# The first four norms: transposing the raw residual and applying the root after the projections

## The chip, the cores and the metric

One Trainium2 chip, one of its cores, one launch. The metric is the device time of that launch in microseconds (us), median of several runs. PE is TensorE (the matrix engine), DVE is VectorE, ACT is ScalarE, POOL is GpSimd, SP is SyncE, which here only issues transfers. SBUF is the on-chip memory that the engines work in, PSUM the eight accumulator banks (128 x 512 f32 each) that PE writes.

## What is computed

A stack over 256 tokens of width 1024, all in float32: retention, gated FFN with a convolution, stick-breaking attention, the same FFN again, a norm, and then a second block (adaptive norm, mLSTM and block attention, mixture of experts). The first four norms, which the change touches, stand ahead of the projections of the first four parts.

```python
def _rmsnorm(x, g):
    xf = x.astype(jnp.float32)
    y = xf * lax.rsqrt(jnp.mean(xf * xf, axis=-1, keepdims=True) + EPS)
    return (y * g.astype(jnp.float32)).astype(x.dtype)

def _retention(h, w_in, w_out):
    ...
    proj = h @ w_in
    ...
    y = jax.nn.silu(g.astype(jnp.float32)) * o
    return y.astype(h.dtype) @ w_out

def _conv_ffn(h, w_up, conv_w, conv_b, w_down):
    u = h @ w_up
    u = lax.conv_general_dilated(u, conv_w[:, None, :].astype(u.dtype), window_strides=(1,),
                                 padding=[(CONV_W - 1, 0)],
    ...
    gate, val = jnp.split(u, 2, axis=-1)
    return (jax.nn.silu(gate) * val) @ w_down

    for i in range(DEPTH):
        j = i // N_MIXERS
        if i % N_MIXERS == 0:
            x = x + _retention(_rmsnorm(x, ret_norm[j]), ret_w_in[j], ret_w_out[j])
        else:
            x = x + _stick_breaking(_rmsnorm(x, sb_norm[j]), sb_w_in[j], sb_w_out[j])
        x = x + _conv_ffn(_rmsnorm(x, ffn_norm[i]), ffn_w_up[i], ffn_conv_w[i],
                          ffn_conv_b[i], ffn_w_down[i])
```

DEPTH is 2: retention stands in the first round, stick-breaking in the second. The factor rsqrt(mean(x*x) + EPS), called the root here, is one number per token. A projection of the normed tokens is therefore the projection of x times g, with each token's outputs multiplied by its root.

## The kernel before

**Products in three passes.** Every weight and every normed activation is split into a rounded high part and a low part (type fp32r), and a product is made as high x high, high x low and low x high. ACT makes the high part of a weight half (`split_high`, L443), DVE the low part (`split_low`, L451), each in two pieces of 128 x 1024. Of the split weights there are two buffers, `w_high` and `w_low`, so the split of half h+2 can begin only when PE is through with half h. A half is 48 matmuls of 256 columns (`by_feature`, L514 to L516; features on partitions, tokens along the columns) or 24 of 512 columns (`by_token`, L529 to L531; tokens on partitions).

**A norm.** ACT squares and sums each 128-token tile as the residual is added (L302), DVE makes mean plus EPS (L309), ACT the square root (L305), DVE the reciprocal (L312) and then the scaled tiles `xn` (L321). PE transposes them by 16 matmuls against the identity into banks 0 to 3 (L337), ACT takes the high part of the transposed tokens times g (L364, eight of 128 x 256) and DVE the low part (L366). The first matmul of the projection waits for the first of four pairs of L366. Ahead of norms 1 and 3 PE runs five matmuls whose result nobody reads (`idle_turns`, L327, 128 x 512); ahead of norm 2 it sums the adaptive gates (L1009, four of 128 x 512).

**After a projection.** Retention's q and k come out with tokens along the columns and DVE rotates them by the cos and sin tables (L1820 to L1824); v and gate come out with tokens on partitions and are copied (ACT L1464, DVE L1831). In the FFN ACT takes a bank of PSUM times the third tap plus the bias (L1528), DVE adds the other two taps in four instructions that read the same bank (L1906, L1912), ACT applies silu (L1534) and DVE multiplies (L1920). In the first FFN PE puts four matmuls of the adaptive weights (`ada_part`, L954) behind every half. Both FFNs have 22 halves.

**Order.** Each engine has one program in order; semaphores join them. SP issues all weight transfers on one queue: ident (the identity), the two halves of x, the first 256 columns of the first weight unit, `small` (gains, biases, taps), the rest of that unit, unit 1 (halves 2 and 3), and from then on unit n when the halves that lay in its slot are split. The other constants, of 576 KB, and the tables for decay, cos and sin, of 1280 KB, are issued behind that wait of unit 2 (L757, L758). DVE waits for them (L1813, L1814) ahead of the splits of the third half. `rqk_free` and `up_free` count the banks that are free again, `norm_xn` the scaled tiles, `x_new` the halves of residual tiles.

## Time and profile before

| | |
|---|---|
| time, median of 3 runs | 1430.35 us (1430.11 to 1430.64) |
| the profiled execution | 1430.92 us, of which its span 1429.2 us |
| PE busy | 1360.0 us, 95% of the span |
| DVE busy | 709.8 us, 50% |
| ACT busy | 557.9 us, 39% |
| POOL busy | 33.9 us, 2% |
| mean granted clock of PE | 0.985 |
| chain that ended last | PE 81%, DVE 7%, DMA 7%, ACT 3%, issue 2% |

Busy shares are means over stages with different limits. The chain is the work that ended last, followed back from the last instruction: in most of the span it lies on PE, and the other engines appear in it where PE stood still for them. Matmuls overlap, so a matmul's listed duration is longer than the distance to the next.

### The profile page before, as it was taken

To read this page: it belongs to the slowest core of one execution; us is meant where nothing else is said; L and a number is where in the kernel's file an instruction comes from. 1 tells how busy PE (TensorE), PEld (TensorE's weight loads), DVE (VectorE), ACT (ScalarE), POOL (GpSimd) and SP (SyncE) were. 2 spreads that over 40 slices of the span, in tenths; PEclk is the share of its full clock that TensorE was granted. 3 is DMA by queue.
4 is the path that set the end of the run, shared out by engine and by line. 5 is a ranking of instruction groups with operands and counts; after the bars stand their busy time and mean duration, and the time that the engine had idled before them with its cause. 6 is when DMAs were issued, how large, how long until landed. Compare 5 with 4: busy or idle time off the path is not lost.

```text
span 1429.2 us, 20105 instructions
## 1 busy us (share of the span) xinstructions
PE 1360.0 (95%) x7982; PEld 983.2 (69%) x7982; DVE 709.8 (50%) x1242; ACT 557.9 (39%) x855; POOL 33.9 (2%) x54
## 2 busy tenths in 40 slices
PE   6999899999999998999999998898999999999996
PEld 6988587888777997899987776764444444444442
DVE  5754546666646444577765765852223223222222
ACT  4344535555545466556554644521111111111111
POOL 1000000111100000000000000000000000000000
PEclk9999999999999999999999999999999999999998
DMA  9557343989943642255645343189999999999994
GB/s 316 180 206 257 118 147 104 311 294 316 354 156 120 209 172 85 68 177 176 236 178 203 111 140 118 60 313 416 427 428 426 430 427 428 429 427 430 428 428 179
DMA packets 112286, 372.64 MB, mean 261 GB/s; under 512 B 4300, under 2 KB 63980, under 8 KB 99552
## 3 DMA queue, kind: packets, MB, share of 16 engines
q1 hardware_dynamic: 104352, 344.07, 62.6%
q0 software_dynamic: 7872, 27.76, 5.7%
q8 instruction: 37, 0.61, 0.2%
q14 instruction: 25, 0.20, 0.0%
HBM read 370.75 MB, written 1.05 MB: 260 GB/s over the span
## 4 chain that ended last, share of the span: by engine, by line
PE 81%; DVE 7%; DMA 7%; ACT 3%; issue 2%; SPq 0%; ACTq 0%; DVEq 0%
PE ps L552 14%; PE ps L1353 13%; PE ps L514 9%; PE ps L515 8%; PE ps L516 8%; PE ps L1374 7%; DMA arena<-in_w_expert_up_dram 5%; PE ps L1336 4%; PE ps L529 3%; PE ps L530 3%; PE ps L531 3%; DVE w_low L451 2%; PE ps L954 2%; PE ps L1380 1%; ACT w_high L443 1%
## 5 line engine op out<-in xcount | busy, mean ns | idle before, releaser
L451 DVE TENSOR_TENSOR w_low<-ring,w_high 128x1024 fp32r<-128x1024 f32 x264 | 311.5, 1222 | 225.6 <-ACT w_high L443 217.2
L443 ACT ACTIVATE w_high<-ring 128x1024 fp32r<-128x1024 f32 x264 | 264.9, 1052 | 228.1 <-PE ps L552 95.1
L514 PE MATMUL ps<-h_high,w_high 128*128 128x256 f32 x1088 | 313.9, 289 | 4.4 <-DVE w_low L451 2.9
L515 PE MATMUL ps<-h_low,w_high 128*128 128x256 f32 x1088 | 309.3, 284 | 0.0
L516 PE MATMUL ps<-h_high,w_low 128*128 128x256 f32 x1088 | 309.1, 284 | 0.0
L514 PEld LDWEIGHTS ps<-h_high,w_high 128*128 128x128 f32 x1088 | 210.2, 193 | 25.0 <-issue 20.9
L515 PEld LDWEIGHTS ps<-h_low,w_high 128*128 128x128 f32 x1088 | 210.3, 193 | 0.0
L516 PEld LDWEIGHTS ps<-h_high,w_low 128*128 128x128 f32 x1088 | 210.1, 193 | 0.0
L1353 PE MATMUL ps<-ring,arena 128*64 128x512 f32 x592 | 176.6, 594 | 6.4 <-issue 1.5
L1353 PEld LDWEIGHTS ps<-ring,arena 128*64 128x64 f32 x592 | 55.4, 137 | 117.4 <-issue 111.8
L552 PE MATMUL ps<-w_high,h_high 128*128 128x512 f32 x304 | 95.8, 397 | 4.7 <-DVE h_low L467 3.0
L1353 PE MATMUL ps<-arena 128*64 128x512 f32 x336 | 98.9, 594 | 0.6 <-DMA arena<-in_w_expert_up_dram 0.6
L552 PE MATMUL ps<-w_low,h_high 128*128 128x512 f32 x304 | 94.2, 391 | 0.0
L552 PE MATMUL ps<-w_high,h_low 128*128 128x512 f32 x304 | 94.1, 391 | 0.0
L1374 PE MATMUL ps<-ring,arena 128*64 128x512 f32 x320 | 92.1, 595 | 0.9 <-ACT arena L1757 0.7
L529 PE MATMUL ps<-w_high,h_high 128*128 128x512 f32 x208 | 82.8, 398 | 2.1 <-DVE w_low L451 1.5
L530 PE MATMUL ps<-w_low,h_high 128*128 128x512 f32 x208 | 81.5, 392 | 0.0
L531 PE MATMUL ps<-w_high,h_low 128*128 128x512 f32 x208 | 81.5, 392 | 0.0
L1745 ACT ACTIVATE arena<-ps,mods 128x128 f32<-128x128 f32 x64 | 24.1, 456 | 134.0 <-PE ps L1336 134.0
L1336 PEld LDWEIGHTS ps<-arena,xn 128*128 128x128 f32 x512 | 61.0, 196 | 15.1 <-issue 12.2
L552 PEld LDWEIGHTS ps<-w_high,h_high 128*128 128x128 f32 x304 | 56.6, 190 | 21.0 <-issue 7.2
L1764 ACT ACTIVATE y_high<-arena 128x512 fp32r<-128x512 f32 x32 | 19.7, 631 | 127.9 <-DVE arena L2355 127.9
(339 smaller groups left out, 1599.5 us busy)
## 6 DMA issues: line engine op xcount, KB each, us to landing
ring<-in_ffn_w_up_dram SPq DMA_DIRECT2D x44, 1024.0 KB, 7.9
ring<-in_w_expert_gate_dram SPq DMA_DIRECT2D x19, 2048.0 KB, 28.6
ring<-in_w_expert_down_dram SPq DMA_DIRECT2D x18, 2048.0 KB, 27.0
ring<-in_w_expert_up_dram SPq DMA_DIRECT2D x18, 2048.0 KB, 26.0
ring<-in_ret_w_in_dram SPq DMA_DIRECT2D x11, 2048.0 KB, 8.0
arena<-in_w_expert_up_dram SPq DMA_DIRECT2D x11, 2048.0 KB, 27.8
ring<-in_ffn_w_down_dram SPq DMA_DIRECT2D x10, 2048.0 KB, 7.9
arena<-in_w_expert_gate_dram SPq DMA_DIRECT2D x10, 2048.0 KB, 25.3
```

Of the source, the lines that this page charges most:

```text
L443: nc.scalar.activation(hi, raw, ACT.Copy).then_inc(hi_done, 1)
L451: last = eng.tensor_tensor(lo, raw, hi.bitcast(F32), ALU.subtract)
L514: nc.tensor.matmul(o, hi, hTh[:, k, :], start=(k == 0), stop=False)
L515: nc.tensor.matmul(o, hi, hTl[:, k, :], start=False, stop=False)
L516: last = nc.tensor.matmul(o, lo, hTh[:, k, :], start=False, stop=(k == KD - 1))
L529: nc.tensor.matmul(o, hi, wh[:, row, :], start=(k == 0), stop=False)
L530: nc.tensor.matmul(o, hi, wl[:, row, :], start=False, stop=False)
L531: last = nc.tensor.matmul(o, lo, wh[:, row, :], start=False, stop=(k == KD - 1))
L552: last = nc.tensor.matmul(ps[:, 4 + 2 * t + half, :], a, w[b][:, cols], start=(first and c == 0), stop=(end and c == 2))
L1336: last = nc.tensor.matmul(ps[:, 4 + half, (k % 4) * P:(k % 4 + 1) * P], xn[:, t, k * P:(k + 1) * P], sel[:, t, :], start=(t == 0), stop=(t ...
L1353: last = nc.tensor.matmul(ps[e * R:(e + 1) * R, 4 + g, :], xg[:, k, e * R:(e + 1) * R], wide[homes[e]][:, k, :], start=(k == 0), stop=(k = ...
L1374: last = nc.tensor.matmul(ps[e * R:(e + 1) * R, 6 + half, :], hgT[:, k, e * R:(e + 1) * R], tall[homes[e]][:, k, half * C:(half + 1) * C], ...
```

## The change

**Norms 0 to 3.** PE transposes the residual itself (`late_pe`), tile by tile and half by half as `x_new` counts them, and ACT and DVE split its product with g as before. The squares of tile 0 stand ahead of ACT's high parts, those of tile 1 and the square root behind the split of the second weight half. DVE then makes the reciprocal and, by two multiplications of the identity, a diagonal matrix of the roots for each tile (`root_diag`). After the second half of the projection (the third in `sb_v`) PE multiplies it by ones into bank 7, which gives the roots along the columns on every partition (`late_rows_pe`, two matmuls of 128 columns), and DVE copies that to `root_rows` (128 x 256).

**Where the root is applied.** In `ret_qk` DVE multiplies cos and sin by the row once. In `ret_vg` and `sb_v` the copies out of PSUM carry the root as a scale. In `sb_qk` the copies become products with the row. In the FFNs DVE writes the bank times the row to `us` in SBUF (128 x 512, one instruction more per half), and taps, bias and convolution read `us`; the bank is free after that one instruction. The row is read only after the splits of half 2, ahead of the evictions of half 0, since it is made after half 1.

**Beside it.** `idle_turns` is three matmuls of 256 columns, behind the transposes. The gate sums of norm 2 are two behind the transposes and two behind half 0 of `sb_v`. SP issues the first weight half ahead of x, and constants and tables ahead of the wait of unit 2. ACT's first function is a copy, so that the table for the square root is loaded behind the first weight split. PE's loop for `ret_qk` and the first round of the FFN loops are written out, as is DVE's FFN loop.

```diff
+        LATE = 4
+        R_BANK = 7
+        root_rows = [carve(14400 if r == 0 else 15000, T) for r in range(LATE)]
+        root_diag = [carve(14656 if r == 0 else 15256, NT, P) for r in range(LATE)]
...
+        def x_ready(eng, r, t, half):
+
+            if r == 0:
+                eng.wait_ge(x_in[t], 16)
+            else:
+                eng.wait_ge(x_new, update(r - 1) - 4 + 2 * t + half + 1)
...
+        def late_square(act, r, t):
+
+            if t == 0:
+                if r == 0:
+                    act.wait_ge(ident_in, 16)
+                nc.scalar.activation(credit[:, 7:8], const[:, 0:1], ACT.Sqrt)
+            x_ready(act, r, t, 1)
+            nc.scalar.activation(xn[:, t, :], x[:, t, :], ACT.Square, accum_out=stat[:, t:t + 1]).then_inc(norm_ss, 1)
+
+        def late_sqrt(act, r):
+            act.wait_ge(norm_ms, r + 1)
+            nc.scalar.activation(stat[:, 4:6], stat[:, 2:4], ACT.Sqrt).then_inc(norm_sd, 1)
+
+        def late_root(dve, link, r):
+
+            dve.wait_ge(norm_ss, NT * (r + 1))
+            nc.vector.tensor_scalar(stat[:, 2:4], stat[:, 0:2], 1.0 / D, EPS, ALU.mult, ALU.add).then_inc(norm_ms, 1)
+            dve.wait_ge(norm_sd, r + 1)
+            link(nc.vector.reciprocal(stat[:, 6:8], stat[:, 4:6]))
+            for t in range(NT):
+                last = nc.vector.tensor_scalar(root_diag[r][:, t, :], ident, stat[:, 6 + t:7 + t], None, ALU.mult)
+            last.then_inc(norm_xn, 1)
+
+        def late_rows_pe(pe, r):
+
+            pe.wait_ge(norm_xn, r + 1)
+            for t in range(NT):
+                last = nc.tensor.matmul(ps[:, R_BANK, t * P:(t + 1) * P], ones, root_diag[r][:, t, :], start=True, stop=True)
+            last.then_inc(norm_rows, 1)
+
+        def late_rows(dve, link, r):
+            dve.wait_ge(norm_rows, r + 1)
+            link(nc.vector.tensor_copy(root_rows[r], ps[:, R_BANK, 0:T]))
+
+        def across(r, n=2):
+            return root_rows[r].unsqueeze(1).broadcast_to([P, n, T])
+
+        def late_pe(pe, r):
+
+            for t in range(NT):
+                for j in range(4):
+                    x_ready(pe, r, t, j // 2)
+                    for k in (2 * j, 2 * j + 1):
+                        last = nc.tensor.transpose(ps[:, j, (k % 2) * T + t * P:(k % 2) * T + (t + 1) * P],
+                                                   x[:, t, k * P:(k + 1) * P], ident)
+                    if t == NT - 1:
+                        last.then_inc(norm_tr, 1)
...
             sp.dma_start(const[:, 0:P], A["const"][:, 0:P]).then_inc(ident_in, 16)
+            first = rows(A["ret_w_in"][0])
+            sp.dma_start(wide[0][:, :, 0:T], first[:, :, 0:T]).then_inc(first_in, 16)
             sp.dma_start(x[:, 0, :], x_tiles[:, 0, :]).then_inc(x_in[0], 16)
             sp.dma_start(x[:, 1, :], x_tiles[:, 1, :]).then_inc(x_in[1], 16)
-            first = rows(A["ret_w_in"][0])
-            sp.dma_start(wide[0][:, :, 0:T], first[:, :, 0:T]).then_inc(first_in, 16)
...
-                if before[n] is not None:
-                    sp.wait_ge(*freed[before[n]])
                 if n == 2:
                     sp.dma_start(const[:, P:], A["const"][:, P:NKEPT]).then_inc(const_in, 16)
                     sp.dma_start(arena[:, ARENA - NCONST + NKEPT:], A["const"][:, NKEPT:]).then_inc(tables_in, 16)
+                if before[n] is not None:
+                    sp.wait_ge(*freed[before[n]])
...
-            norm_pe(pe, 0)
...
+            late_pe(pe, 0)
+
+
+            for h in range(8):
+                buf = split_ready(pe, "ret_qk", h)
+                if h >= 4:
+                    pe.wait_ge(rqk_free, h - 3)
+                by_feature(h % 4, buf, None if h else 0).then_inc(wide_mm, 1)
+                if h == 1:
+                    pe.wait_ge(const_in, 16)
+                    late_rows_pe(pe, 0)
...
+                        if isinstance(i, int) and h == 1:
+                            late_rows_pe(pe, 2 * l + 1)
+
+                four(0)
+                with pe.Fori(1, 5) as i:
+                    four(i)
...
-            norm_pe(pe, 1, 5)
+            late_pe(pe, 1)
+            idle_turns(3, 4, T)
             pe.wait_ge(ada_c, 1)
-            pe.wait_ge(const_in, 16)
             ffn(0)
...
+            def gate_sums(g, q):
                 for half in range(2):
                     last = nc.tensor.matmul(ps[:, 4 + 2 * g + half, :], ones,
                                             ada_acc[:, q * D + half * C:q * D + (half + 1) * C],
                                             start=True, stop=True)
-            last.then_inc(ada_gsum, 1)
-            norm_pe(pe, 2)
+                last.then_inc(ada_gsum, 1)
+
+            pe.wait_ge(ada_ev, 2 + NB)
+            late_pe(pe, 2)
+            gate_sums(0, 2)
 
 
             for h in range(4):
                 buf = split_ready(pe, "sb_v", h)
                 by_token(2 * (h // 2), buf, h % 2, 2 if h < 2 else None).then_inc(wide_mm, 1)
+                if h == 0:
+                    gate_sums(1, 5)
+                if h == 2:
+                    pe.wait_ge(ada_gate, 4)
+                    late_rows_pe(pe, 2)
...
-            norm_act(act, 0)
+            act.wait_ge(ident_in, 16)
             nc.scalar.activation(credit[:, 3:4], const[:, 0:1], ACT.Copy).then_inc(rvg_fa, 2)
             split_high(act, "ret_qk", 0)
+            late_square(act, 0, 0)
             act.wait_ge(small_in, 16)
             split_norm(act, 0, 0)
             split_high(act, "ret_qk", 1)
+            late_square(act, 0, 1)
+            late_sqrt(act, 0)
             for h in range(2, count["ret_qk"]):
                 split_high(act, "ret_qk", h)
+            act.wait_ge(norm_xn, 1)
...
-                                             ACT.Copy).then_inc(rvg_fa, 1)
+                                             ACT.Identity, scale=stat[:, 6:7]).then_inc(rvg_fa, 1)
...
+                    act.wait_ge(up_free, off + ((FP + 4) * l + 4 + 2 * b + j + 1))
                     for gv in range(2):
                         at = (l * 2 + gv) * FP
                         last = nc.scalar.activation(
-                            cv[:, j, gv * T:(gv + 1) * T], ps[:, (2 * b + j) % 4, gv * T:(gv + 1) * T], ACT.Identity,
+                            cv[:, j, gv * T:(gv + 1) * T], us[:, j, gv * T:(gv + 1) * T], ACT.Identity,
...
+            def late_norm(r, phase):
+                split_high(act, phase, 0)
+                late_square(act, r, 0)
+                split_norm(act, r, 0)
+                split_high(act, phase, 1)
+                late_square(act, r, 1)
+                late_sqrt(act, r)
+
+            late_norm(1, "up0")
...
-            norm_dve(dve, link, 0)
-            dve.wait_ge(small_in, 16)
-            nc.vector.memset(credit[:, 0:1], 0.0).then_inc(rqk_free, 4)
-            nc.vector.memset(credit[:, 2:3], 0.0).then_inc(rvg_fv, 2)
             nc.vector.memset(hT[:, 0, :], 0.0).then_inc(ada_zero, 1)
             split_low(dve, "ret_qk", 0)
+            dve.wait_ge(small_in, 16)
             split_norm(dve, 0, 1)
             split_low(dve, "ret_qk", 1)
+            late_root(dve, link, 0)
             cos, sin = k_("cos"), k_("sin")
-            dve.wait_ge(const_in, 16)
-            dve.wait_ge(tables_in, 16)
             for q in range(8):
                 u = ps[:, q % 4, :]
                 split_low(dve, *(("ret_qk", q + 2) if q < 6 else ("ret_vg", q - 6)))
+                if q == 0:
+                    late_rows(dve, link, 0)
+                    dve.wait_ge(tables_in, 16)
+                    for table in (cos, sin):
+                        pair_of = table.rearrange("p (b t) -> p b t", b=2)
+                        link(nc.vector.tensor_tensor(pair_of, pair_of, across(0), ALU.mult))
+                    nc.vector.memset(credit[:, 2:3], 0.0).then_inc(rvg_fv, 2)
...
+                def pair(n):
+                    c, u = cv[:, n % 2, :], us[:, n % 2, :]
...
+                    def scaled():
+                        wide_done(dve, halves[f"up{l}"] + n + 1)
+                        nc.vector.tensor_tensor(u.rearrange("p (b t) -> p b t", b=2),
+                                                ps[:, n % 4, :].rearrange("p (b t) -> p b t", b=2), across(r), ALU.mult)\
+                            .then_inc(up_free, 1)
+
+                    if n:
+                        scaled()
+                    if n + 2 < FP:
+                        split_low(dve, f"up{l}", n + 2)
+                    elif n + 2 == FP:
+                        split_low(dve, f"down{l}", 0)
                     else:
...
+                        src_low(dve, f"down{l}", hff, 0)
+                        split_low(dve, f"down{l}", 1)
+                        src_low(dve, f"down{l}", hff, 1)
+                    if n == 0:
+                        late_rows(dve, link, r)
+                        scaled()
+                    dve.wait_ge(up_id, FP * l + n + 1)
+                    dve.wait_ge(up_free, (FP + 4) * l + 4 + n + 1)
...
+                    dve.wait_ge(up_si, FP * l + n + 1)
                     nc.vector.tensor_tensor(hff[:, n, :], c[:, 0:T], c[:, T:C], ALU.mult).then_inc(up_h, 1)
...
+                for n in range(FP):
+                    pair(n)
```

The order on ACT at the start of the program, before; `credit` is a scratch column, `stat` holds the sums and roots:

```order
L299 ACT_TABLE_LOAD
L299 ACTIVATE credit<-const 128x1
L302 ACTIVATE xn,stat<-x_hT 128x1024 x2
L305 ACTIVATE stat<-stat 128x2
L1450 ACTIVATE credit<-const 128x1
L443 ACTIVATE w_high<-ring 128x1024 x2
L364 ACTIVATE h_high<-ps,small 128x256 x8
```

The same place in the changed kernel, with its own line numbers:

```order
L1526 ACT_TABLE_LOAD
L1526 ACTIVATE credit<-const 128x1
L502 ACTIVATE w_high<-ring 128x1024 x2
L312 ACT_TABLE_LOAD
L312 ACTIVATE credit<-const 128x1
L314 ACTIVATE xn,stat<-x_hT 128x1024
L423 ACTIVATE h_high<-ps,small 128x256 x8
L502 ACTIVATE w_high<-ring 128x1024 x2
L314 ACTIVATE xn,stat<-x_hT 128x1024
L318 ACTIVATE stat<-stat 128x2
```

The weight split now stands ahead of a second table load and of one square; the other square and the root have moved behind the second split.

The order on DVE in `ret_qk`, before, from the splits of the second and third half to that of the fourth:

```order
L451 TENSOR_TENSOR w_low<-ring,w_high 128x1024 x4
L1820 TENSOR_TENSOR xn<-ps,arena 128x512
L1821 TENSOR_TENSOR xn<-ps,arena 128x256
L1822 TENSOR_TENSOR xn<-ps,arena 128x256
L1824 TENSOR_TENSOR arena<-xn 128x512
L451 TENSOR_TENSOR w_low<-ring,w_high 128x1024 x2
```

The first row ends with the split of the third half, behind which the first rotation follows. The changed kernel, from the split of the third half on:

```order
L510 TENSOR_TENSOR w_low<-ring,w_high 128x1024 x2
L339 COPY arena<-ps 128x256
L1902 TENSOR_TENSOR arena<-arena 128x512 x2
L1903 MEMSET credit 128x1
L1905 TENSOR_TENSOR xn<-ps,arena 128x512
L1906 TENSOR_TENSOR xn<-ps,arena 128x256
L1907 TENSOR_TENSOR xn<-ps,arena 128x256
L1909 TENSOR_TENSOR arena<-xn 128x512
L510 TENSOR_TENSOR w_low<-ring,w_high 128x1024 x2
```

Between the split and the first rotation the copy of the row and the two table products have come in.

The order on DVE at the start of the first FFN, before, where the last rows are the loop's first evictions:

```order
L366 SCALAR_TENSOR_TENSOR h_low<-ps,small,h_high 128x256 x8
L451 TENSOR_TENSOR w_low<-ring,w_high 128x1024 x2
L1922 UNCONDITIONAL_BRANCH
L1922 ISA
L451 TENSOR_TENSOR w_low<-ring,w_high 128x1024
L450 REGISTER_ALU
L451 TENSOR_TENSOR w_low<-ring,w_high 128x1024
L1903 ISA
L1906 ISA
L1906 SCALAR_TENSOR_TENSOR arena<-ps,small,arena 128x255
```

The split of half 2 is followed by the evictions of half 0. The changed kernel, from the diagonal matrices on:

```order
L327 TENSOR_SCALAR arena<-const,stat 128x128 x2
L510 TENSOR_TENSOR w_low<-ring,w_high 128x1024 x2
L339 COPY arena<-ps 128x256
L1980 TENSOR_TENSOR arena<-ps,arena 128x512
L2003 SCALAR_TENSOR_TENSOR arena<-arena,small 128x255 x2
L2003 SCALAR_TENSOR_TENSOR arena<-arena,small 128x254 x2
L2012 TENSOR_TENSOR arena<-arena 128x256
L1980 TENSOR_TENSOR arena<-ps,arena 128x512
L510 TENSOR_TENSOR w_low<-ring,w_high 128x1024 x2
L2003 SCALAR_TENSOR_TENSOR arena<-arena,small 128x255 x2
```

The split of half 3 (the second L510) stands behind the whole eviction of half 0, and that stands behind the copy of the row (L339), which PE makes after half 1.

## Rows read from the trace of the kernel before

**Rows 1.** page: busy time of an engine; then GB/s in 40 equal slices

```profile
PE 1360.0 (95%) x7982; PEld 983.2 (69%) x7982; DVE 709.8 (50%) x1242; ACT 557.9 (39%) x855; POOL 33.9 (2%) x54
...
GB/s 316 180 206 257 118 147 104 311 294 316 354 156 120 209 172 85 68 177 176 236 178 203 111 140 118 60 313 416 427 428 426 430 427 428 429 427 430 428 428 179
```

**Rows 2.** waits of PE, whole span: engine line <- releaser: us in total, times, longest

```profile
PE ps L337 <- DVE xn L321: 11.1, 4, 9.9
```

**Rows 3.** timeline of the start: start us, us, engine line op out<-in xcount [idle <-releaser]

```profile
0.87 1.28 ACT L299 ACT_TABLE_LOAD   x1 [0.87 <-PEq L2448]
...
5.21 1.06 ACT L302 ACTIVATE xn<-x_hT 128x1024 f32<-128x1024 f32 x1 [2.16 <-DMA x_hT<-in_x_dram]
...
9.54 2.00 ACT L443 ACTIVATE w_high<-ring 128x1024 fp32r<-128x1024 f32 x2 [1.30 <-DMA ring<-in_ret_w_in_dram]
...
9.94 3.64 PE L337 MATMUL ps<-const,xn 128*128 128x128 f32 x16 [9.94 <-DVE xn L321]
...
10.64 2.35 DVE L451 TENSOR_TENSOR w_low<-ring,w_high 128x1024 fp32r<-128x1024 f32 x2
...
11.45 3.01 ACT L364 ACTIVATE h_high<-ps,small 128x256 fp32r<-128x256 f32 x8
...
12.91 3.22 DVE L366 SCALAR_TENSOR_TENSOR h_low<-ps,small,h_high 128x256 fp32r<-128x256 f32 x8
...
13.92 0.55 PE L514 MATMUL ps<-h_high,w_high 128*128 128x256 f32 x1 [0.34 <-DVE h_low L366]
```

**Rows 4.** timeline of the first projection, tables and the fifth weight half

```profile
18.81 0.43 SPq L758 DMA_DIRECT2D arena<-in_const_dram  x1
...
26.76 2.36 DVE L451 TENSOR_TENSOR w_low<-ring,w_high 128x1024 fp32r<-128x1024 f32 x2 [8.37 <-DMA arena<-in_const_dram]
...
31.15 2.36 DVE L451 TENSOR_TENSOR w_low<-ring,w_high 128x1024 fp32r<-128x1024 f32 x2
...
36.84 2.01 ACT L443 ACTIVATE w_high<-ring 128x1024 fp32r<-128x1024 f32 x2 [8.43 <-DMA ring<-in_ret_w_in_dram]
```

**Rows 5.** two windows of 10 us: window, length, busy (x) by engine, PEclk, DMA share, GB/s

```profile
26.00:36.00 10.00, 7.13 (x48) 6.93 (x47) 8.64 (x12) 2.00 (x2) 1.60 (x3) 0.83 1.03 340
...
903.00:913.00 10.00, 7.39 (x59) 6.64 (x57) 5.63 (x10) 1.97 (x3) 0.00 (x0) 1.00 0.05 20
```

**Rows 6.** timeline around norm 1, PE, DVE and ACT

```profile
224.49 4.45 PE L327 MATMUL ps<-const 128*128 128x512 f32 x10
...
224.69 1.29 DVE L576 TENSOR_TENSOR x_hT<-ps,x_hT 128x512 f32<-128x512 f32 x2 [0.73 <-PE ps L552]
...
229.30 1.97 PE L337 MATMUL ps<-const,xn 128*128 128x128 f32 x16 [0.36 <-DVE xn L321]
...
230.00 3.02 ACT L364 ACTIVATE h_high<-ps,small 128x256 fp32r<-128x256 f32 x8 [2.40 <-PE ps L337]
...
231.90 0.35 PE L514 MATMUL ps<-h_high,w_high 128*128 128x256 f32 x1 [0.62 <-DVE h_low L366]
```

**Rows 7.** timeline around norm 2, PE and DVE

```profile
451.65 3.67 PE L1009 MATMUL ps<-arena,const 128*128 128x512 f32 x8 [1.47 <-DVE x_hT L576]
...
457.69 0.47 PE L529 MATMUL ps<-w_high,h_high 128*128 128x512 f32 x1 [0.62 <-DVE h_low L366]
...
462.08 2.48 DVE L1958 TENSOR_TENSOR gates<-ps,gates 128x512 f32<-128x512 f32 x4
```

**Rows 8.** timeline of one up-projection half of the second FFN, ACT and DVE

```profile
600.44 2.01 ACT L443 ACTIVATE w_high<-ring 128x1024 fp32r<-128x1024 f32 x2 [1.76 <-PE ps L516]
...
602.36 1.00 ACT L1528 ACTIVATE arena<-ps,small 128x256 f32<-128x256 f32 x2
...
605.34 0.42 ACT L1534 ACTIVATE arena<-arena 128x256 f32<-128x256 f32 x1 [1.98 <-DVE arena L1912]
...
601.53 2.36 DVE L451 TENSOR_TENSOR w_low<-ring,w_high 128x1024 fp32r<-128x1024 f32 x2 [2.92 <-ACT w_high L443]
...
607.25 1.23 DVE L451 TENSOR_TENSOR w_low<-ring,w_high 128x1024 fp32r<-128x1024 f32 x1 [0.85 <-ACT w_high L443]
```

124 lines of the change are left out of this document (43 added, 81 removed).

## Prediction

> **What bounds the kernel now.** I read the page first: PE is busy 95% of the span, DVE half of it [rows 1]. So time is won only where PE stands still, runs work that nobody needs, or runs at the lower clock, and I went on to the waits of PE: the transposes of the norms waited 11.1 us in four pieces for DVE's scaled tiles, 9.9 of them at the start [rows 2]. The timelines then show what PE does around each norm. At norm 1 the projection's last matmul is followed at 224.49 by five idle turns, then by the transposes at 229.30, and the first useful matmul starts at 231.90, 7.4 us later [rows 6]. Norm 3 has the same form. At norm 2 the gate sums fill part of the same chain [rows 7]. At the start the first matmul is at 13.92 [rows 3], and halves 2 and 3 of `ret_qk` suffer from the tables: DVE waits 8.37 us for them ahead of the split at 26.76 [rows 4]. From 26 to 36 us PE is busy 7.13 of 10 us, idle for 2.87, at a mean granted clock of 0.83 [rows 5].
>
> **Start and `ret_qk`.** Landings: tile 0 of x was there at 5.21 and the first weight half at 9.54, 1.5 MiB in 4.33 us between them [rows 3]. With the weight half (1 MiB) in place of tile 0 (0.5 MiB) at the head, it lands at about 5.21 + 1.44 = 6.65. ACT's split takes 2.00, to 8.65; the second table load 1.28, to 9.95; one square 1.06 with some tenths around it; so ACT begins the high parts at 11.4, where it began before at 11.45 [rows 3]. The table load eats what the earlier weight gives. But DVE's low weight part, which ran from 10.64 for 2.35 and held L366 back to 12.91, is now done by 10.1. In norm 1 the first matmul comes 1.90 behind ACT's first high part (230.00 to 231.90) [rows 6]; here that is 13.3: **-0.6**. The transposes run earlier, with a longer hole behind them. At the start 16 of them took 3.64 us, against 1.97 in norm 1, so PE was at the lower of its two clock levels (1.2 GHz); I charge **+0.3** for a later rise, with ends at -0.7 and +2.
>
> The tables now follow unit 1 in the queue and land before they are needed. The idle 2.87 goes, and with it the low clock: 0.17 of 10 us [rows 5], **-2.87** and **-1.7**. In their place stands the row. Two 128-column products cost PE what its idle turns show: ten records in 4.45 us are five matmuls of 512 columns [rows 6], so 128 columns take 0.22 and two 0.45: **+0.45**. Behind it DVE copies the row (about 0.4), multiplies two tables (about 0.7 each, with waits 1.6 together) and rotates, which takes 2.03 (29.12 to 31.15), and only then splits half 3 in 2.36 [rows 4]. With hand-over times that is 6.8 us behind the row, and PE has half 2 for 5.72 of them (601.53 to 607.25, one half's period) [rows 8]: a new wait of **+1.05**. Sum of this stage: -3.4. On the clock of the run: half 1 ends at 26.0, half 2 at 32.2, half 3 starts at 33.25 and ends at 39.0.
>
> **Norm 1.** Residual tile 0 is ready when the projection ends, so eight transposes run from 224.5 to 225.5. DVE adds tile 1 in two pieces from 224.69 to 225.98 [rows 6]; each piece releases four transposes of 0.12. The first pair is done at 225.8, ACT starts at 226.0, and 1.90 later, at 227.9, the projection can start. PE ends its transposes at 226.7 and runs three turns of 256 columns, 1.33 us, to 228.05. Against 231.90 that is **-3.85**; the idle turns cost 0.15 of it. The row adds **+0.45**.
>
> Then comes what the change adds by its order. DVE reads the row only after half 1, and behind it stand the eviction of half 0 and the split of half 3, on DVE and on ACT both. I lay it from the row matmuls' start R. Row copied at R+1.1; scaled bank at R+1.9; ACT's bias pass from R+2.1. From that pass to silu took 2.98 before (602.36 to 605.34), silu 0.42, from ACT's split to DVE's 1.09 (600.44 to 601.53), DVE's split 2.36 [rows 8]. Half 3 is ready at R+8.9. PE has 0.45 for the row, 5.72 to 5.9 for half 2 and, in this FFN, 1.0 for the adaptive weights: it arrives at R+7.4. **+1.5**. Norm 1 gives -1.9.
>
> **Norm 2.** The same chain, but the gate sums are real work of 3.67 us [rows 7]. Half of them now runs while ACT and DVE split, so with the transposes done at 452.2 (as in norm 1, 2.2 behind the projection) and two sums of 1.84 together the first product starts at 454.05; the other half (1.84) and the row (0.45) follow it: 456.35 in place of 457.69, **-1.35**. DVE adds the gates (2.48, [rows 7]) behind the second half of the sums and ahead of a weight split, which costs PE 0 to 0.7; I take +0.05. -1.3.
>
> **Norm 3.** -3.85 and +0.45 as in norm 1; without adaptive weights PE arrives at R+6.2 and waits **+2.65**: -0.75. Whether PE comes back at the lower clock is open: after 2.87 idle it did, after 2.61 (903 to 913 us, clock 1.00) it did not [rows 5]. The price was 1.7; the new gap lies between the two, and I take half: **+0.85**. +0.1 for norm 3.
>
> **Steady state.** The FFNs get one DVE instruction more per half, 0.6 us apart from its neighbour. In the second FFN DVE stood idle for 0.85 ahead of a split in a period of 5.72 [rows 8], so it fits by 0.25, and the first FFN has 1.0 more. Scaled copies in `ret_vg`, `sb_v` and `sb_qk` take the place of unscaled ones; I take them at nothing, covered by PE's halves, with +1 as the upper end. The experts' stage streams weights at 427 GB/s [rows 1]; its first loads are released by work behind the norms, so it moves forward with them.
>
> **Sum.** -3.4 - 1.9 - 1.3 + 0.1 = -6.5. The profiled execution took 1430.92, a span of 1429.2 and 1.7 around it; it lies 0.6 above the median, so the same difference taken from the median 1430.35 gives **1423.8**.
>
> **The rivals.**
>
> *The waits behind the row are smaller, or low-clock stretches elsewhere vanish.* If ACT and DVE catch up within half 2, the three waits (1.05, 1.5, 2.65) and the clock term fall away by half or more: -6.5 - 3 to -6, 1418 to 1421. Against it: in-order queues, and each term of the chain comes from a row. Chance 0.12.
>
> *The row's waits cost clock too.* Three new gaps of 1 to 2.7 us, the hole at the start, and all later gaps shifted against the clock's changes: each fall costs 1.7 [rows 5]. Two more give 1427.2, and 1426 to 1428.5 is this case's range. Chance 0.15.
>
> *The fifth weight half is late.* In the trace it was issued after the tables and ACT could start on it only at 36.84, after an idle 8.43 [rows 4], with POOL's transfers in flight. If it lands there again, it is split 3.45 later, at 40.3, while PE now wants it at 39.0: +1.3, 1425.1. For it: POOL's transfers do not move. Against it: the tables are out of the way, 1280 KB that were ahead of it. Chance 0.10. The Trainium skill, page "DMA: Bandwidth & Descriptors", section "Queues, rings and completion order", says that a DMA engine takes turns between the queues that have work, packet by packet; by that rule POOL's queue keeps its share whatever SP puts ahead, which is this rival, and its sum would be -5.2. No row separates the two queues' shares here.
>
> *The experts' stream swallows it.* If the 427 GB/s stretch [rows 1] ended at a fixed time, the end would stay at 1430.4. Against it: nothing ties it to a time, each slot is refilled when PE has used it. Chance 0.05.
>
> *Slower.* DVE becomes the bound of the second FFN: `scaled` reads a repeated row and PSUM and stands between silu's product and the next split, on a loop of ACT and DVE that has 0.25 to spare. If the loop's period grows beyond 5.72 by d, PE loses d in each of some 19 halves behind the first wait. To lose the 6.5 and 2.9 more, d must be 0.5, so `scaled` would have to cost 0.75 more than the 0.6 that I give it, over 1.35. Two-input instructions of 128 x 1024 cost 1.18 a piece [rows 8], so 512 columns at half that rate would just reach it. Chance 0.04.
>
> **Chances and range.** The forecast itself, 1421.5 to 1426, has 0.54; the five rivals 0.12, 0.15, 0.10, 0.05 and 0.04. A measurement of this kernel can tell about 0.2%, 2.9 us, from no change. Faster by more than that, below 1427.5: 0.54 + 0.12 + 0.10 + two thirds of 0.15, less a little for what I have not seen, 0.85; within it 0.11; slower 0.04. The range 1419.5 to 1427.5 takes in the late half, most of the clock case, half of the small waits, and leaves out about 2 in 10.
>
> **What would show it.** In the profile of the changed kernel: the first product near 13.3; no idle PE and full clock at 26 us, but a wait of about 1 us ahead of half 3 of `ret_qk`; the first product of norm 1 3.85 us earlier against the projection's end; a wait of 1.5 us ahead of half 3 in the first FFN and of 2.65 in the second, with the clock falling behind the second or not; DVE some 13 us busier in 22 halves of each FFN, with no PE wait in the steady state. If PE waits for DVE's low part in every half of the second FFN, the slower case holds; if PE's gaps are gone and the end has not moved, the experts' stream held it. I am wrong in the sum if any wait behind the row is off by more than 1 us.

## The result, and the profile of the changed kernel

The changed kernel takes **1419.17 us** (median of 4 executions, 1417.32 to 1419.43), the kernel before beside it 1430.23: ratio 0.992, 95% interval 0.9907 to 0.9932. The forecast was 1423.8 with a range from 1419.5. So the sign was right, the gain of 11.1 us was 1.7 times the forecast 6.5, and the time lies 0.3 us under the range. With the later repetitions it is 1419.36 over 15 executions against 1430.57 over 56.

The page of the changed kernel: its span, the busy time of the engines, and GB/s in 40 slices.

```profile
span 1417.5 us, 19885 instructions
...
PE 1353.1 (95%) x7990; PEld 981.7 (69%) x7990; DVE 738.1 (52%) x1291; ACT 562.7 (40%) x856; POOL 33.3 (2%) x54
...
GB/s 318 206 204 241 122 145 129 323 310 320 341 166 132 212 146 60 76 192 187 248 166 178 134 119 119 60 342 419 426 427 427 429 428 428 429 429 428 429 428 192
```

PE's busy time fell by 6.9 of the 11.7 us that the span lost, and DVE's grew by 28.3 [rows 1]. The experts' stream has the same 427 GB/s and simply ends earlier.

**The start**, timeline of the changed kernel (start us, us, engine, operation):

```profile
6.80 2.00 ACT L502 ACTIVATE w_high<-ring 128x1024 fp32r<-128x1024 f32 x2 [2.48 <-DMA ring<-in_ret_w_in_dram]
...
8.26 3.65 PE L350 MATMUL ps<-const,x_hT 128*128 128x128 f32 x16 [8.26 <-DMA x_hT<-in_x_dram]
8.82 1.28 ACT L312 ACT_TABLE_LOAD   x1
...
11.27 3.01 ACT L423 ACTIVATE h_high<-ps,small 128x256 fp32r<-128x256 f32 x8
...
13.22 0.55 PE L573 MATMUL ps<-h_high,w_high 128*128 128x256 f32 x1 [1.32 <-DVE h_low L425]
```

The weight is split from 6.80 (forecast 6.65), the high parts begin at 11.27 (11.4), the first product at 13.22 (13.3), against 13.92 in [rows 3]. Behind it the clock rises later than before: the matmuls of 256 columns, 0.21 us apart at first, come 0.12 apart from 15.48 on in the kernel before and from 17.20 on in the changed one (timelines of PE, before and then changed):

```profile
15.13 0.40 PE L516 MATMUL ps<-h_high,w_low 128*128 128x256 f32 x1
...
15.48 0.28 PE L515 MATMUL ps<-h_low,w_high 128*128 128x256 f32 x1
15.60 0.28 PE L516 MATMUL ps<-h_high,w_low 128*128 128x256 f32 x1
```

```profile
16.77 0.41 PE L574 MATMUL ps<-h_low,w_high 128*128 128x256 f32 x1
16.99 0.37 PE L575 MATMUL ps<-h_high,w_low 128*128 128x256 f32 x1
17.20 0.28 PE L573 MATMUL ps<-h_high,w_high 128*128 128x256 f32 x1
```

In this the same matmuls go from 0.70 ahead of before to 0.41 behind. The granted clock does not show it: the profile gives 1.00 from 12 to 19 us in both traces, though a distance of 0.21 is what the same matmuls have near 601 us, where it shows the lower level.

**`ret_qk`**, timelines of DVE, PE and ACT:

```profile
22.15 2.36 DVE L510 TENSOR_TENSOR w_low<-ring,w_high 128x1024 fp32r<-128x1024 f32 x2 [3.42 <-ACT w_high L502]
27.20 0.42 DVE L339 COPY arena<-ps 128x256 f32<-128x256 f32 x1 [2.69 <-PE ps L334]
27.66 1.42 DVE L1902 TENSOR_TENSOR arena<-arena 128x512 f32<-128x512 f32 x2
...
31.32 2.36 DVE L510 TENSOR_TENSOR w_low<-ring,w_high 128x1024 fp32r<-128x1024 f32 x2
...
33.74 0.39 PE L573 MATMUL ps<-h_high,w_high 128*128 128x256 f32 x1 [0.83 <-DVE w_low L510]
...
39.86 2.01 ACT L502 ACTIVATE w_high<-ring 128x1024 fp32r<-128x1024 f32 x2 [4.84 <-PE ps L575]
```

The tables no longer stand ahead of the split of half 2 (at 22.15 where it was at 26.76), the row is copied at 27.20, and with the table products and the rotation behind it this holds the split of half 3 back to 31.32; PE waits 0.83 for it. The split at 39.86 is that of the fifth half: released by PE, not by a transfer as at 36.84 in [rows 4]. That weight is not late.

**The norms.** Norm 1, then norm 2, then the two places of norm 3 with its first product in the kernel before (the row of L514), all timelines:

```profile
219.65 2.20 PE L350 MATMUL ps<-const,x_hT 128*128 128x128 f32 x16
219.85 1.29 DVE L635 TENSOR_TENSOR x_hT<-ps,x_hT 128x512 f32<-128x512 f32 x2 [0.74 <-PE ps L611]
...
221.07 3.03 ACT L423 ACTIVATE h_high<-ps,small 128x256 fp32r<-128x256 f32 x8 [0.77 <-PE ps L350]
...
221.69 1.46 PE L386 MATMUL ps<-const 128*128 128x256 f32 x6
...
222.96 0.36 PE L573 MATMUL ps<-h_high,w_high 128*128 128x256 f32 x1
```

```profile
442.74 2.20 PE L350 MATMUL ps<-const,x_hT 128*128 128x128 f32 x16
...
444.78 1.88 PE L1076 MATMUL ps<-arena,const 128*128 128x512 f32 x4
...
446.10 0.80 PE L588 MATMUL ps<-w_high,h_high 128*128 128x512 f32 x1
```

```profile
579.88 0.35 PE L573 MATMUL ps<-h_high,w_high 128*128 128x256 f32 x1
...
600.12 0.39 PE L573 MATMUL ps<-h_high,w_high 128*128 128x256 f32 x1 [2.17 <-DVE w_low L510]
```

```profile
594.14 0.35 PE L514 MATMUL ps<-h_high,w_high 128*128 128x256 f32 x1 [0.62 <-DVE h_low L366]
```

In norm 1 the first product starts 3.3 us behind the transposes' first, where it was 7.4 behind the projection's end [rows 6]. Against the matmuls ahead of it, it moved forward by 4.08 in norm 1, 4.30 in norm 2 (half of whose gate sums now follow it) and 4.06 in norm 3.

**The clock.** Busy time, length and granted clock (the number behind POOL's) of four windows of the changed kernel; then of two of the kernel before:

```profile
26.00:36.00 10.00, 9.17 (x77) 8.97 (x76) 8.46 (x15) 4.02 (x4) 2.00 (x4) 1.00 0.78 239
175.00:185.00 10.00, 8.97 (x40) 7.47 (x41) 4.76 (x7) 4.20 (x7) 0.62 (x1) 1.00 0.38 131
550.00:560.00 10.00, 10.00 (x54) 8.63 (x53) 4.78 (x5) 6.90 (x9) 0.00 (x0) 1.00 0.00 1
600.00:606.00 6.00, 5.88 (x36) 5.88 (x37) 5.80 (x11) 3.30 (x5) 0.00 (x0) 0.72 0.82 265
```

```profile
175.00:185.00 10.00, 7.69 (x26) 6.22 (x27) 4.47 (x8) 2.67 (x5) 0.75 (x1) 0.66 0.64 239
550.00:560.00 10.00, 7.49 (x38) 5.54 (x39) 2.11 (x4) 7.88 (x10) 0.00 (x0) 0.66 0.66 210
```

This is what the forecast did not have. The kernel before runs 10 us near 176, and 10 us near 551, at a mean of 0.66: two thirds of each at the lower of the two levels (1.2 in place of 2.4 GHz), which costs up to 3.4 us each time, less where PE waits anyway. In this execution of the changed kernel the first is absent, and the second is shorter and lies at 542 (clock 0.91 from 540 to 560, against 0.83 from 545 to 565 before). The waits ahead of both are the same in both traces: 1.4 at most in the retention, and 3.2 at L1110 (before L1035).

**Where the 11.7 us went.** Shift of the same matmul from one trace to the other (profiled executions: span 1429.2 to 1417.5):

| stage | forecast | measured |
|---|---|---|
| start and `ret_qk` | -3.4 | -2.6 |
| low clock near 176 | 0 | -2.2 |
| norm 1, with its wait | -1.9 | -2.4 |
| norm 2 | -1.3 | -1.6 |
| low clock near 551 | 0 | -1.3 |
| norm 3, with wait and clock | +0.1 | +0.2 |
| from 606 us to the end | 0 | -1.8 |
| sum | -6.5 | -11.7 |

The first line is read at the first matmul of the retention, which stands behind `ret_qk` and `ret_vg` and ahead of the stretch near 176 (timelines of PE, before and changed):

```profile
152.32 1.02 PE L906 MATMUL ps<-arena 128*128 128x256 f32 x4
```

```profile
149.71 0.81 PE L969 MATMUL ps<-arena 128*128 128x256 f32 x3
```

The four stages that the forecast had priced sum to -6.4 here, almost its -6.5; the other -5.3 lie in the three lines that it had at nothing. In the last line, stretches at the low clock near 845 (-1.5), near 898 (+1.6) and near 955 (nothing in the end) almost cancel. What is left of it is mostly a wait for an expert's weights, -1.1 by shift (PE's waits, before and changed; 1.1 again in the next execution traced of the changed kernel):

```profile
PE ps L1353 <- DMA x_hT<-in_w_expert_gate_dram: 1.3, 1, 1.3
```

```profile
PE ps L1429 <- DMA x_hT<-in_w_expert_gate_dram: 0.3, 1, 0.3
```

To see this for many executions I use, for each, its span and its mean granted clock. Their product is a full-clock time: it leaves out what the lower level costs (and, a little too much, idle time within it; the clock is given to 0.001, or 1.4 us an execution). Over all executions:

| kernel | n | median us | mean us | mean clock | span x clock |
|---|---|---|---|---|---|
| before | 56 | 1430.57 | 1430.56 | 0.9859 | 1408.7 |
| changed | 15 | 1419.36 | 1419.74 | 0.9883 | 1401.4 |

Work and waits: **-7.3**. Clock: 0.0024 of 1420, **-3.4**. The forecast says -5.65 for the first and -0.85 (-1.7 + 0.85) for the second. Its +0.3 for the late rise at the start belongs to the first, since the granted clock does not show that rise.

### The profile page after: what moved, and what is told of

Its sections match the earlier page's. It is cut to its first block, busy times and chain, and to the rows that moved or that the text cites. A ratio compares the mean times of both kernels' runs of the same rounds, so it can differ in the third digit from the quotient of the medians.

```text
span 1417.5 us, 19885 instructions
## 1 busy us (share of the span) xinstructions
PE 1353.1 (95%) x7990; PEld 981.7 (69%) x7990; DVE 738.1 (52%) x1291; ACT 562.7 (40%) x856; POOL 33.3 (2%) x54
## 3 DMA queue, kind: packets, MB, share of 16 engines
HBM read 370.75 MB, written 1.05 MB: 262 GB/s over the span
## 4 chain that ended last, share of the span: by engine, by line
PE 81%; DVE 7%; DMA 6%; ACT 4%; issue 2%; SPq 0%; ACTq 0%; DVEq 0%
PE ps L611 14%; PE ps L1429 13%; PE ps L573 8%; PE ps L574 8%; PE ps L575 8%; PE ps L1450 7%; DMA arena<-in_w_expert_up_dram 5%; PE ps L1412 4%; PE ps L588 3%; PE ps L589 3%; PE ps L590 3%; DVE w_low L510 2%; PE ps L1017 2%; PE ps L1456 1%; ACT w_high L502 1%
## 5 line engine op out<-in xcount | busy, mean ns | idle before, releaser
L510 DVE TENSOR_TENSOR w_low<-ring,w_high 128x1024 fp32r<-128x1024 f32 x264 | 311.4, 1221 | 175.6 <-ACT w_high L502 175.5
L2003 DVE SCALAR_TENSOR_TENSOR arena<-arena,small 128x254 f32<-128x254 f32 (+1 forms) x176 | 77.0, 478 | 4.3 <-ACT arena L1609 2.8
L2437 DVE SCALAR_TENSOR_TENSOR arena<-arena,ps 128x512 f32<-128x512 f32 x16 | 17.9, 1116 | 101.8 <-PE ps L1429 101.8
```

The source lines that it names most:

```text
L510: last = eng.tensor_tensor(lo, raw, hi.bitcast(F32), ALU.subtract)
```

## Experiments

**Theory A**: the forecast's mechanisms are right, and the rest is low-clock stretches of the kernel before that the change only happens to meet less often. **Theory B**: the change removed more work or waits than I saw. **Theory C**: the place of the work in time decides where the clock falls.

**The row of roots after half 0 instead of half 1**, which moves DVE's copy and the first scaled bank ahead of the split of half 2:

```diff
-                if h == 1:
+                if h == 0:
                     pe.wait_ge(const_in, 16)
                     late_rows_pe(pe, 0)
...
-                    if n:
-                        scaled()
+                    if n == 0:
+                        late_rows(dve, link, r)
+                    scaled()
```

> The changed kernel with the row of roots made after half 0 in place of half 1 in ret_qk and both FFNs, and in the FFNs read ahead of the split of half 2. Theory (the waits of 0.83, 1.13 and 2.17 us ahead of half 3 come from where the row stands in the order, and the 2.17 us also made the clock fall, 1.7 us): all three waits fall below 0.3 us, no low clock behind norm 3, time 1419.2 - 0.8 - 1.1 - 2.2 - 1.7 = 1413.4, if nothing else moves. Rival (the roots are not ready after half 0, since squares, root and diagonal matrices end only 5.5 us behind the first product): PE waits for the diagonal matrices instead, and the time stays between 1417 and 1421.

Measured 1417.10 (1412.21 to 1418.72, ratio 0.987 to 0.9913). All three waits ahead of half 3 are gone from the trace: no wait of PE on `w_low` is left between 14 and 700 us. The low-clock stretch behind norm 3 is gone with them, but those near 174 and 545 are back at full length. The same kernel again:

> e1_row_after_half0 once more, unedited, to place its scattered runs (1412.2 to 1418.7 at a clock of 0.990 to 0.985): a median of 1413 to 1418, with 4 us or more between its fastest and slowest run, two groups by the clock, and time times clock some 4 to 5 us below that of the changed kernel (its three waits are gone).

Measured 1413.83, and all four executions within 0.6 us, clock 0.989 or 0.990. The expected scatter did not come: on another chip the kernel ran in one group. Over both, 8 executions: 1414.1, span x clock 1397.0, 4.4 below the changed kernel. The three waits sum to 0.83 + 1.13 + 2.17 = 4.1. So the waits were real and cost about what the trace says. The 1413.4 that was expected for the first of the two runs came out only with the second: the clock, 0.987 in the mean of the first and 0.990 of the second, decides 3 us of it.

**All moved by 2.7 us, before:** three idle matmuls of 512 columns ahead of `ret_vg`.

```diff
+            pe.wait_ge(const_in, 16)
+            for _ in range(3):
+                nc.tensor.matmul(ps[:, 7, :], ident, const[:, 0:C], start=True, stop=True)
             with pe.Fori(0, 4) as i:
```

> The kernel before with three matmuls of 512 columns, read by nobody, ahead of ret_vg: 2.67 us of work added and nothing else. Theory (the low-clock stretches at 176 and 551 us in the trace of before do not belong to their idle times alone but also to when these come, and the changed kernel lost them by moving them): the profile shows at least one of these stretches gone or shorter, and the time grows by less than 2.7 us, by +1.5 to -1.5. Rival (the changed kernel lost them by what it changed): all stretches stay, and the time is 1430.2 + 2.7 = 1432.9.

Measured 1432.72 (1430.17 to 1436.36, ten executions), clock 0.986 as before, 0.983 to 0.988 within one kernel, and span x clock +2.6. Moving everything by 2.7 did not change the mean clock, and near 176 and 551 the clock fell as before (at 181 and 557).

**The parts of the change alone.** The kernel before with the tables issued ahead of the wait for unit 2's slot, and the changed kernel with x ahead of the weight half and the tables behind that wait:

```diff
+                if n == 2:
+                    sp.dma_start(const[:, P:], A["const"][:, P:NKEPT]).then_inc(const_in, 16)
+                    sp.dma_start(arena[:, ARENA - NCONST + NKEPT:], A["const"][:, NKEPT:]).then_inc(tables_in, 16)
                 if before[n] is not None:
                     sp.wait_ge(*freed[before[n]])
-                if n == 2:
-                    sp.dma_start(const[:, P:], A["const"][:, P:NKEPT]).then_inc(const_in, 16)
-                    sp.dma_start(arena[:, ARENA - NCONST + NKEPT:], A["const"][:, NKEPT:]).then_inc(tables_in, 16)
```

> The kernel before with the constants and tables issued ahead of the wait of unit 2, one part of the change alone. Theory (the idle 2.87 us ahead of half 2 of ret_qk and the 1.7 us of low clock behind it are the tables' alone): both go, -4.3 to -4.6 up to the end of ret_qk, 1425.8 if no stretch of low clock later moves. Rival (the fifth weight half is then late, or POOL's transfers hold the tables up): a new wait of 1 to 2 us at half 4, time 1427 to 1430.

> The changed kernel with x ahead of the first weight half and the tables behind the wait of unit 2, as before. Theory (the tables' place is worth the idle wait and its low clock, the weight's place little since the square root's table load stands in its way): DVE waits for the tables near 26.7 us, behind the split of half 2 and no longer ahead of it, so PE's wait ahead of half 3 stays near 0.8 to 1.3 us; first product 2 to 3 us later than 13.2, since the weight split of 2.0 us and the table load of 1.28 follow the weight's landing at 9.5. Time 1419.2 + 2 to + 4. Rival (most of the gain at the start is the tables' place): + 5 us or more.

Measured 1424.85 (ratio 0.9938 to 0.9971) and 1425.26 (0.9941 to 0.9974). The tables alone give the idle time and the clock of [rows 5] back, as the window of that kernel shows:

```profile
26.00:36.00 10.00, 10.00 (x85) 10.00 (x84) 8.49 (x13) 4.01 (x4) 1.42 (x3) 1.00 1.05 350
```

That is -5.7, of which span x clock explains 3.1 (2.87 of idle time was forecast) and the clock the rest (0.9877; one fall in [rows 5] is worth 1.7). With the old transfers the first product is at 15.76, 2.5 later than in the changed kernel:

```profile
15.76 0.55 PE L573 MATMUL ps<-h_high,w_high 128*128 128x256 f32 x1 [7.10 <-DVE h_low L425]
```

The second kernel lies 6 us above the changed one where 2 to 4 were expected, in the range of its rival. Over the ten executions that it has with a later run it is 5.1 above in time, and 1.9 in span x clock: the rest is clock. The two parts, -5.7 and -5.3 from the 1430.57 of before (-6.1 with the ten), add up to the whole within 1 us.

**The changed kernel again, unedited:**

> The changed kernel, unedited, once more. Theory A (the 4.6 us by which the change beat my forecast are stretches at the low clock that come and go between executions, not something the change made): another execution has its stretches elsewhere or of another length; the profile's stretches sum to between 24 and 41 us in place of 23.9, span less half of them stays within 0.7 of 1405.5, and the median of many runs lies between 1418 and 1421, the single runs 2 to 4 us apart. Theory B (the change itself did away with the stretches near 176 and 551 us, because no other pattern of idle time stands ahead of them): both are absent again, the stretches sum to 23 to 25 us, and the runs stay within 0.5 us of 1419.2.

Measured 1419.09, single executions 1418.51 to 1424.30. The profiled one is that of 1424.30, with a span of 1422.6 and a clock of 0.984, and it has both stretches again, with the same waits ahead of them (windows of that execution):

```profile
173.00:183.00 10.00, 8.53 (x30) 6.74 (x31) 3.60 (x6) 2.67 (x5) 0.76 (x1) 0.66 0.56 205
545.00:555.00 10.00, 9.15 (x46) 6.67 (x45) 3.02 (x5) 7.57 (x10) 0.00 (x0) 0.66 0.63 206
```

That speaks for A: the same program, with and without them. Where they are in both traces, the kernels' spans differ by 1429.2 - 1422.6 = 6.6. That this is the forecast's sum is in part chance: this execution has the lower mean clock (0.984 against 0.985), and span x clock of the two differs by 8.0.

**The slower rival: the product with the row computed twice.**

```diff
                         wide_done(dve, halves[f"up{l}"] + n + 1)
+                        for _ in range(1):
+                            link(nc.vector.tensor_tensor(u.rearrange("p (b t) -> p b t", b=2),
+                                                    ps[:, n % 4, :].rearrange("p (b t) -> p b t", b=2), across(r), ALU.mult))
```

> The changed kernel with the product of each up half with the row of roots computed twice on DVE in both FFNs (same result): 0.69 and a wait on its own result more per half. Tests my slower rival (DVE bound in the second FFN, deciding from 0.75 us more in that place, worth 0.5 us in each of 19 halves). If DVE's busy sum (some 5.4 us a half, here 6.15) sets the pace from there on, the second FFN's halves go from 5.74 to 6.2 us and the kernel loses 8 to 10 us: 1427 to 1429. If the loop of ACT and DVE still has the slack that the waits suggest, it loses 0 to 3: 1419 to 1422. The first FFN, 1 us a half longer on PE, loses nothing in either.

Measured **1432.10** (1430.05 to 1438.29): 13 us lost, more than either expectation gave. Span x clock rose by 5.9, and the clock fell to 0.9832, another 7. The 5.9 are not in the steady state. Waits of PE in the second FFN, of this kernel (engine, line, releaser: sum, times, longest):

```profile
PE ps L611 <- DVE h_low L526: 4.2, 1, 4.2
PE ps L573 <- DVE w_low L510: 3.6, 1, 3.6
```

These are one wait each: ahead of half 3 (2.17 in the changed kernel) and ahead of the down projection (1.5), with 2.6 against 1.13 in the first FFN: 1.4 + 2.7 + 1.5 = 5.6. Between them PE's halves run back to back. DVE's own waits in that FFN show why, first in the changed kernel, then in this one:

```profile
DVE w_low L510 <- ACT w_high L502: 9.1, 17, 1.4
```

```profile
DVE w_low L510 <- ACT w_high L502: 0.6, 1, 0.6
```

DVE stood idle 9.1 us over 17 halves, 0.53 a half; the second product (0.69) uses all of it, and next to nothing is left. The period did not grow with two products of 1.38 us in all, so the 1.35 at which the forecast put the slower case was too low; that the brink lies close above is argued, not measured. A shortage of DVE showed at the stage's ends and in the clock and not in the period.

**Without the idle turns of norms 1 and 3** (the two calls taken out):

```diff
-            idle_turns(3, 4, T)
```

> The changed kernel without the three idle matmuls of 256 columns ahead of the transposes of norm 1 and norm 3 (0.3 us of PE each group, work that nobody needs). If they only fill time in which PE would wait for the scaled tiles: no change of work, 1418 to 1420. If the filled idle time keeps the clock up: one or two stretches at the low clock of 3.41 us more behind the norms, +1.7 to +3.4, 1420 to 1423.

Measured 1422.13 (1419.68 to 1424.19, four executions, clock 0.984 to 0.990), span x clock -1.0. The intervals of the ratios, 0.9917 to 0.9957 and 0.9907 to 0.9934, overlap. No low-clock stretch appeared directly behind norm 1. Inconclusive: span x clock of the four executions runs from 1398.7 to 1403.7, so neither a cost of the turns (0.6 us in both places was expected) nor what they give back in clock is resolved.

**Idle time filled.** Idle matmuls of 512 columns: one in each of three waits of the retention, three ahead of the wait of 3.2 at L1110. First with the early row, then in both kernels of the comparison:

```diff
+                if h == RH - 1:
+                    idle_turns(1, 0)
                 if h >= 1:
                     ret_turn(h - 1)
+            idle_turns(1, 0)
             ret_turn(RH - 1)
+            idle_turns(1, 0)
             pe.wait_ge(r_ta, RH)
...
+                if g == 6:
+                    idle_turns(3, 1)
                 if g >= 2:
                     pe.wait_ge(s_a, g - 1)
```

> Row of roots after half 0 (as in e1_row_after_half0), and idle matmuls put into PE's waits in the retention (one in each of three waits) and ahead of the wait near 930 us of the kernel before (three). If idle time of 1 to 3 us on PE brings the low clock behind it: the stretches near 173, near 833 to 845 and near 941 us go or get shorter, sum of stretches 15 to 27 us in place of 34.1, time 1411 to 1416, at most 1.5 us of it spoilt by an idle matmul that ends late. If the stretches are set by something else: 1416 to 1419 as before.

> e9_rows_early_gaps_filled once more on the chip of e10 and e11: 1411 to 1413, clock 0.990 to 0.991, runs within 3 us. Against e11 it shows the three waits ahead of half 3 alone: 4 to 5 us faster.

> The kernel before with the idle matmuls of e9 alone (one of 512 columns in each of three waits of the retention, three ahead of the wait near 542 us), no work moved. If the 3 to 6 us between an execution with and one without the stretches near 176 and 551 us are set by the idle time ahead of them: the mean granted clock of the runs rises from 0.986 to 0.989 or 0.990, the stretches near 176, 551 and 845 are gone, and the time falls by 3 to 6, to 1424.5 to 1427.5, with runs within 2 us of each other. If the stretches come from elsewhere: 1430 to 1432, clock 0.985 to 0.987.

> The changed kernel with the same idle matmuls. The changed kernel already runs at 0.989 in most executions, so they have less to give: clock 0.990 to 0.991 in every run, 1415.5 to 1418.5. Against e10 this compares the two kernels with the accidental stretches out of both: the difference should be the work and waits of my forecast with the rest of the clock, -6 to -8.5 us, not -11. If the difference is still -10 to -12, the change saves more work or waits than I have found in the trace.

Measured in this order 1411.68, 1413.18, 1425.44 and 1417.27. All lie in the expected ranges but the second, which is 0.2 above its own; it is 4.1 below the changed kernel with filled waits on the same chip, where 4 to 5 were expected. Over all executions of each kernel:

| kernel | n | median us | mean us | mean clock | span x clock |
|---|---|---|---|---|---|
| before, filled | 12 | 1425.44 | 1426.19 | 0.9892 | 1409.0 |
| changed, filled | 5 | 1417.27 | 1417.75 | 0.9896 | 1401.3 |
| row early | 8 | 1414.10 | 1415.07 | 0.9884 | 1397.0 |
| row early, filled | 9 | 1411.83 | 1412.67 | 0.9904 | 1397.5 |

The kernel before gains 5 us of median from matmuls whose results nobody reads (ratio 0.9959 to 0.9983), with its full-clock time unchanged. In its trace the two stretches are at full clock (windows near 176 and 551):

```profile
175.00:185.00 10.00, 8.89 (x40) 6.18 (x40) 5.29 (x10) 3.37 (x7) 0.76 (x1) 1.00 0.76 285
550.00:560.00 10.00, 8.68 (x56) 6.93 (x57) 3.71 (x5) 8.34 (x11) 0.00 (x0) 1.00 0.66 211
```

The same holds in all four traces with filled waits, while of 13 traces without, 8 have the first stretch and all 13 have one near 541 to 557. So the idle time ahead is a condition for both, shown by taking it away; given the idle time, the first comes in some executions and not in others. Changed against before, both filled and on one chip, is -8.2 in medians, -8.4 in means (give or take 2, from the spread of the 12 and 5 executions) and -7.7 in full-clock time, with clocks 0.0004 apart: at the edge of the expected -6 to -8.5, and not -11. So A holds for what the clock gave, and B is worth 1.5 to 2 us. What A says of chance is weaker: the changed kernel meets the stretches less often than before, and the runs do not say why.

**Place in time.** The changed kernel moved by the same three idle matmuls, its variant with the old transfers again, and itself, on one chip:

> The changed kernel with three idle matmuls of 512 columns between ret_qk and ret_vg: 2.7 us of PE that move all that follows and change no wait behind it. If the place of the work against the chip's own rhythm decides whether the clock falls near 173 and 545 us: the mean granted clock leaves 0.988 or 0.989, most likely to 0.985 or 0.986 as in e4, where everything came 2.5 later too, and the time is 1424 to 1427. If the place does not matter: the clock stays at 0.988 and the time is 1421.8, 2.7 above the changed kernel, within 1.2.

> e4_change_with_old_transfers once more, beside the unedited changed kernel on one chip. There its clock was 0.985 against 0.988 of the changed kernel on two other chips. If that difference belongs to the program: again 0.984 to 0.987 and 1424 to 1427, 5 to 7 us above the changed kernel. If it belonged to the chip or the day: the clock of the changed kernel, 0.988, and only its 2.5 us of later start, 1420.5 to 1422.5.

> The changed kernel, unedited, as the reference for the two others of this call: 1418 to 1421, clock 0.987 to 0.989, time of most runs within 1 us of 1419.2 and, if the one run of 1424.3 at 0.984 was no accident, one or two runs near 1424.

Measured 1423.30, 1423.58 and 1419.56. The mean clock of the shifted kernel is 0.9875 (0.985 to 0.989, six executions), +2.2 in full-clock time; its median is 3.7 above the kernel unshifted, 1 more than the matmuls themselves, between the two expectations. Its trace has no stretch near 173, although all is moved there. The variant with the old transfers came out 4.0 above the changed kernel beside it, between its two expectations; it has 0.9864 over its 10 executions, and no stretch near 178 in the new trace where the earlier one had it. The changed kernel had one execution of 1424.42 at 0.984 among six, so two of 15 in all, against 24 of 56 executions of the kernel before at 0.985 or less. Theory C finds no support: a shift changes the odds by little if at all.

## Why the prediction missed

By its own steps:

- **Start: right, but for the clock.** 13.22 for 13.3. The late rise of the clock was +1.1 where I took +0.3 (range to +2).
- **Tables: right.** The idle 2.87 and the clock's fall are gone, in this kernel and with the tables moved alone; by shift they were worth 3.0 and 1.45 (2.87 and 1.7 forecast). The wait behind the row, +1.05, is listed with 0.83 and costs 1.1 by shift: a listed duration reaches over the start of the next matmul, so PE loses 0.1 to 0.3 more than a listed wait.
- **Norm 1: -3.85 measured -4.08, wait +1.5 listed with 1.13, 1.2 by shift.** Three idle turns of 256 columns are listed with 1.46; from the first of them to the first product it is 1.27 (forecast 1.33).
- **Norm 2: -1.35 measured -1.6.** The first product came 4.30 earlier (forecast 3.64), and the sums' other half and the row gave 2.7 back (2.29).
- **Norm 3: -3.85 measured -4.06, wait +2.65 listed with 2.17, 2.4 by shift, clock +0.85 measured 1.45** (1.7 by the clock, 0.72 over 6 us in the window from 600). I had put half a chance on the fall; here, and in the executions traced of the unedited kernel, it came in two of three.
- **The row: +0.45, right.** The four records at 26.55 are listed with 0.60, but the product behind them starts 0.36 later and the next one another 0.08 late: 0.44. In norm 1 it is 0.45 by shift.
- **Steady state: right.** `scaled` took 0.69 for 0.6 and PE waited for it nowhere; the room was 0.53 a half, not the 0.25 that I read from one period [rows 8]. The slower rival was weaker than its text has it: 512 columns at half the rate of [rows 8] are 1.18, which is short of its own 1.35.
- **The fifth half: the rival fell.** ACT took it at 39.86 straight behind PE. The Trainium skill's rule ("DMA: Bandwidth & Descriptors", section "Queues, rings and completion order"), by which POOL's queue keeps its turn in each DMA engine, may hold; it did not make this weight late, and no run here separates the queues' shares.
- **What failed**: the step **Sum**, which took the difference from the time of the kernel before as if all that this time holds stayed, but for the one fall of the clock at 29 us that I had priced. Low-clock stretches elsewhere stood at nothing in it, and so did everything behind norm 3. In the two traces these two hold the whole miss: -2.2 near 176, -1.3 near 551 and -1.8 behind 606 us. Over many executions the clock gives -3.4 where I had -0.85, and work and waits -7.3 where I had -5.65. Only the rival "low-clock stretches elsewhere vanish" had the sign of it, at a chance of 0.12 with 1418 to 1421, where the time fell; its other half, smaller waits, is not what happened. Two things in the trace spoke for a wider range downwards. A mean clock of 0.985 over 1429 us is some 43 us at the low level, some 7 of them at the very end, where PE has no matmul, and only 3.4 in the fall that [rows 5] show. And of the waits ahead of the two stretches one, 3.2, was longer than the 2.87 behind which [rows 5] show a fall. I asked this of my new waits and not of the old ones.
- **Luck and the smaller terms**: that the priced stages sum to -6.4 in this pair is in part luck. The clock cost 1.4 more than I took at the start and behind norm 3, less the 0.25 that the fall at 29 us gave too little; norm 1 gave 0.5 more than forecast, norm 2 0.3, norm 3 without its clock 0.5 and `ret_qk` 0.2, by earlier first products and waits 0.3 shorter in norms 1 and 3. No wait behind the row was off by more than 1 us, the sign that I had named for a wrong sum; the sum was wrong without it.

**Left open**: why the fall near 174 is rarer in the changed kernel than before (absent in two of its three traces, while clocks of 0.985 or less come in 2 of 15 executions against 24 of 56). The same waits stand ahead, a shift does not decide it, filling them ends it.

## What to carry to other kernels

Before you sum an edit, read the granted clock over the whole span and set aside what the low level costs: where the stretches follow idle time, they may belong to an execution and not to the program, and a gain can be some us larger or smaller than its work. Compare kernels by span times mean granted clock beside the time. And where work is put between two splits on an in-order engine, place it a half earlier if its input is there: the row after half 0 in place of half 1 was worth 4 to 5 us, and with the waits filled (1411.8, nine executions) beats the changed kernel by 7.5.
